# A nine-stage transformer kernel: value projections taken in pairs, and sums of squares as rounded products

## The chip, the cores and the metric

The program runs on one core of a Trainium2 chip. The metric is the device time of one execution in microseconds (us). TensorE (PE) multiplies, VectorE (DVE), ScalarE (ACT) and GpSimd (POOL) work on elements, SyncE (SP) issues most transfers. Each engine runs its own instructions in order and waits on semaphores for the others.

## The reference

512 tokens of width 1024 pass nine stages, all in float32, each after an RMS norm and added to the residual `x`: SSD and GLA (sharing one norm), SwiGLU, MLA, SwiGLU, retention, SwiGLU, stick-breaking attention, SwiGLU.

```python
def rms_norm(x, w):
    y = xf * lax.rsqrt(jnp.mean(xf * xf, axis=-1, keepdims=True) + NORM_EPS)
# MLA: 16 heads, low-rank q and kv
q = (rms_norm(cq, q_lora_norm) @ w_uq)          # per head 64 + 32 rope
kv = (rms_norm(ckv, kv_lora_norm) @ w_ukv)      # per head k 64, v 64
q_nope, q_rope, k_nope = ...                    # each normed, rope applied
p = softmax(causal(scale * (q @ k.T)));  o = p @ v
# stick-breaking: 16 heads of 64
q, k = rms_norm(q), rms_norm(k)
weight = exp(log_sigmoid(z) + later)            # later: sum of log_sigmoid(-z) over later keys
```

## The kernel before, in words

Activations lie transposed (feature on the partition, 512 tokens along the row) in eight tiles of 128x512. A float32 operand is split in a rounded high part (type fp32r) and the rest; a product is three TensorE products, high by high, high by low and low by high (`product`, L402; `features2`, L435). Other products take float32 operands as they are: among them the sums of squares of a norm (`norm`, L731, with `ones` as weights, one per 512 tokens), the mean of retention's output (L1308), MLA's k mean (L1154) and the k mean of stick-breaking (L1335).

Weights come in one stream of chunks, two in flight. SP loads chunk c into `raw` slot c % 2, POOL splits it (L716 rounds, L704 subtracts) into `w_hi`, `w_lo` once TensorE has counted the chunk before in that slot as used (`s_used`), and TensorE waits for the split.

**Norm.** ACT squares the tiles, DVE adds them into `norm_sq[:, 0]` (`squares_added`, L1872), TensorE sums over the partitions behind the next stage's first projection, ACT takes Ln and Exp (L1473, L1474).

**MLA.** Eight pairs of heads; pair u attends while pair u+1 is projected, normed and rotated. TensorE's order in a pair: `scores` of both heads (L1161 to L1166), `proj_q` (L402, 18 products), `max_turned` (L1173), `scores_turned` of head 0 (L1180 to L1185), `q_means` (L1149, L1150), `scores_turned` of head 1, `proj_k` (6 products of 512 columns), `proj_v` (24 products whose moving side is the v weight, 128 columns), `k_mean` (L1154), `weighted` twice (L1192). PSUM banks 0 to 5 hold scores and outputs, 6 and 7 the projections and means in turn. DVE norms both q heads at once: scale (L2228), two turned products for the rope (L2192), the cosine product (L2234), the sum (L2235), then k (`k_ready`, L2242), whose end lets the next `scores` start (`s_mq`). q's rstd comes from ACT, Ln per head (L1703) and one Exp for both (L1704). Before pair 0 stand the low-rank latents and their norms; DVE also fills both k buffers with the rope part (L2214) and copies four constants (L2285 to L2289).

**Retention.** Per head DVE adds four squares (L2354), and the mean is L1308.

**Stick-breaking.** Eight pairs in a like pipeline. In a pair TensorE does scores, q and k projections (banks 6, 7), `later_sums` of head 0 (L1377, L1382), `means` of the next pair (q in bank 6, L1332, L1333; k in bank 7, L1335), the first half of `proj_v` (bank 6, L1345), `later_sums` of head 1, the second half, `weighted` (bank 7, L1395), `turn_v` (L1353). DVE between the two `later_sums` splits head 1's softplus (`softplus_split`, L2406, L2407).

**End.** Once all tiles of `x` are updated (L1915) SP stores them in one transfer (L690).

Of the kernel before, what the change touches and what calls it, by code (L numbers as in the profile page):

```python
# [16 lines left out]
ALU = mybir.AluOpType  # L17
# [108 lines left out]
def weight_chunks(i, layers):  # L126
# [20 lines left out]
    for name in layers:  # L147
# [18 lines left out]
        if name == "mla":  # L166
# [4 lines left out]
            for u in range(8):  # L171
                wq = i["w_uq"][0][:, 192 * u:192 * u + 192]
                q = cols_of(*(rope_spread(wq[:, 96 * e:96 * e + 64], wq[:, 96 * e + 64:96 * e + 96]) for e in range(2)))
                q = block(q, slice(0, 384), slice(0, 256))

                kv = i["w_ukv"][0][:, 256 * u:256 * u + 256].reshape(256, 2, 2, 64).transpose(0, 2, 1, 3).reshape(256, 256)
                kv = block(kv, slice(0, 256), slice(0, 256))
                out.append(np.concatenate([q, kv], axis=1))
# [34 lines left out]
STAGE_WIDTHS = {"ssd": [384] + [2048] * 15, "gla": [2048] * 15, "mla": [2048] * 3 + [1280] * 8 + [2048] * 4,  # L213
# [65 lines left out]
def build_program(nc, x_in, weights, general_in, param_in, phase_in, out, general_at, param_at, phase_at, layers):  # L279
# [6 lines left out]
    with ExitStack() as stack:  # L286
# [168 lines left out]

        used[0] = 0
# [11 lines left out]
        def phase_const(stage, name):  # L468
# [130 lines left out]
                                                sem("mla_latent_means"), sem("mla_latent_rstd"))  # L599
        s_mkxs, s_msl = sem("mla_k_rope_square"), sem("mla_q_squares_low")  # L600
        s_mh = sem("mla_latents_normed")
# [27 lines left out]
                                                   sem("ret_mean"), sem("ret_rstd"), sem("ret_o_normed"))  # L629
        r_oo = [r_q[:, 0, :], r_q[:, 1, :], r_k[:, 0, :], r_k[:, 1, :]]  # L630
# [17 lines left out]
        k_sqh, k_sql = a_hi[:, 7, :], a_lo[:, 7, :]  # L648
# [15 lines left out]
        def _(sp):  # L664
# [61 lines left out]
        def _(pe):  # L726
            pe.sem_inc(s_used, 2)

            def norm(name):
                pe.wait_ge(s_acc, norm_of[name])  # L730
                pe.matmul(ps[:, norm_bank(name), :], ones, norm_sq[:, 0, :], start=True, stop=True).then_inc(s_mean, 1)  # L731
# [261 lines left out]
            def gla(c0):  # L993
# [104 lines left out]
                residual_begun("gla", (4, 5))  # L1098
                mean(hd)
                residual_begun("gla", range(6), 1)  # L1100

            def mla(c0):
# [26 lines left out]
                def kv_weights(par, k, at):  # L1129
                    at += 768 + 256 * k  # L1130
                    return [b[:, (c0 + 3 + par) % 2, at:at + P] for b in (w_hi, w_lo)]

                def proj_k(w, par):
                    pe.wait_ge(s_mln, 2 * w + 1)
                    product(pe, ps[:, 6, :], [(*kv_weights(par, k, 0), h_hi[:, k, :], h_lo[:, k, :])
                                              for k in range(2)]).then_inc(s_mpk, 1)

                def proj_v(w, par):
                    pe.wait_ge(s_mln, 2 * w + 2)
                    for tb in range(TB):  # L1140
                        s = slice(tb * P, (tb + 1) * P)
                        mm = product(pe, ps[:, 7, s], [(h_hi[:, k, s], h_lo[:, k, s], *kv_weights(par, k, P))
                                                       for k in range(2)])
                    mm.then_inc(s_used, 1)

                def q_means(w):
                    for e in range(2):
                        pe.wait_ge(s_msl, 2 * w + e + 1)
                        pe.matmul(ps[:, 6 + e, :], m_blkq, m_sqh[:, e, :], start=True, stop=False)  # L1149
                        pe.matmul(ps[:, 6 + e, :], m_blkq, m_sql[:, e, :], start=False, stop=True).then_inc(s_mm, 1)  # L1150
# [46 lines left out]
                def pair(u, par, first, ahead):  # L1197
# [5 lines left out]
                    pe.wait_ge(s_mv, u + 1)  # L1203
# [7 lines left out]
                    if not ahead:  # L1211
# [1276 lines left out]
```

## Time and profile before

| | |
|---|---|
| three timed runs | 2897.52, 2898.31, 2899.02 us |
| median | 2898.31 us |
| the profiled execution's own time | 2898.93 us |
| its span, first to last instruction | 2897.1 us |
| busy: TensorE, VectorE, ScalarE, GpSimd | 99%, 45%, 20%, 64% |
| mean granted TensorE clock | 0.995 |

The profile is of one execution; times in its rows count from the start of the span. A product's duration there is its way through the array and is longer than the distance from one product's start to the next one's; where products follow each other, the distance is what counts. A float32 product that is not rounded shows as two records.

### The profile page before, as it was taken

The page shows a single profiled execution, that of the slowest core. Times are in us where ns is not written, and L with a number is a line of the kernel's source. Part 1 is how long each engine was busy: PE and PEld are TensorE (multiplying, and loading weights), DVE is VectorE, ACT ScalarE, POOL GpSimd, SP SyncE. Part 2 cuts the span into 40 slices and gives each one's busy share as a digit, 9 for nine tenths or more (in the row PEclk, how much of TensorE's full clock was granted, in tenths as well). Part 3 has the DMA queues.
Part 4 walks back from the last instruction along what each step waited for, and adds up shares of the span by engine and source line. Part 5 has one row for each costly group of instructions (what it writes and reads, how often), then busy time and mean ns, then how long its engine had stood idle before and what let it go on. Part 6 is the DMA issues. An engine that isn't in the chain of part 4 may idle for free.

```text
span 2897.1 us, 36332 instructions
## 1 busy us (share of the span) xinstructions
PE 2864.6 (99%) x13536; PEld 2326.3 (80%) x13536; DVE 1301.5 (45%) x1506; ACT 565.8 (20%) x821; POOL 1848.9 (64%) x1822
## 2 busy tenths in 40 slices
PE   9999999999989999999999999999999999999998
PEld 6778888888867778888888888788888777788887
DVE  5765545414355654414444223444244455543241
ACT  4550221000124541000111101210001445300000
POOL 5557548777752238777775565677777544677775
PEclk9999999999999999999999999999999999999999
DMA  4112213232220102222232222222322111222322
GB/s 152 61 60 88 74 57 111 80 108 100 84 85 28 38 29 87 92 103 102 80 125 85 74 94 81 73 100 80 105 95 91 69 63 54 72 95 84 106 92 89
DMA packets 38583, 242.35 MB, mean 84 GB/s; under 512 B 4288, under 2 KB 4672, under 8 KB 16608
## 3 DMA queue, kind: packets, MB, share of 16 engines
q1 hardware_dynamic: 37296, 237.19, 23.5%
q10 hardware_dynamic: 1200, 3.96, 0.4%
q8 instruction: 60, 0.98, 0.1%
q14 instruction: 27, 0.22, 0.0%
HBM read 239.04 MB, written 2.10 MB: 83 GB/s over the span
## 4 chain that ended last, share of the span: by engine, by line
PE 94%; DVE 3%; ACT 1%; DVEq 1%; issue 0%; ACTq 0%; DMA 0%; SPq 0%
PE ps L402 67%; PE ps L435 13%; PE ps L1345 1%; PE ps L1161 1%; PE ps L1301 1%; PE ps L1180 1%; PE ps L1382 1%; PE ps L1362 1%; PE ps L1395 1%; PE ps L1377 1%; PE ps L1291 1%; DVEq L2262 0%; DVEq L1857 0%; PE ps L1053 0%; DVE scr L2235 0%
## 5 line engine op out<-in xcount | busy, mean ns | idle before, releaser
L716 POOL CAST w_hi<-raw 128x512 fp32r<-128x512 f32 (+1 forms) x909 | 677.5, 761 | 1030.7 <-PE ps L402 836.7
L704 POOL TENSOR_TENSOR w_lo<-raw,w_hi 128x512 fp32r<-128x512 f32 (+1 forms) x909 | 1220.0, 1354 | 0.1
L402 PE MATMUL ps<-h_hi,w_hi 128*128 128x512 f32 x1904 | 751.7, 395 | 3.3 <-DVE h_lo L1868 3.0
L402 PE MATMUL ps<-h_hi,w_lo 128*128 128x512 f32 x1904 | 742.0, 390 | 0.0
L402 PE MATMUL ps<-h_lo,w_hi 128*128 128x512 f32 x1904 | 741.5, 389 | 0.0
L402 PEld LDWEIGHTS ps<-h_hi,w_hi 128*128 128x128 f32 x1904 | 357.8, 188 | 80.8 <-issue 5.3
L402 PEld LDWEIGHTS ps<-h_hi,w_lo 128*128 128x128 f32 x1904 | 357.6, 188 | 75.7
L402 PEld LDWEIGHTS ps<-h_lo,w_hi 128*128 128x128 f32 x1904 | 357.9, 188 | 75.1 <-issue 2.9
L402 PE MATMUL ps<-a_hi,w_hi 128*128 128x512 f32 x816 | 319.7, 392 | 2.2 <-issue 1.4
L402 PE MATMUL ps<-a_hi,w_lo 128*128 128x512 f32 x816 | 318.3, 390 | 0.0
L402 PE MATMUL ps<-a_lo,w_hi 128*128 128x512 f32 x816 | 318.1, 390 | 0.0
L1896 DVE TENSOR_TENSOR scr<-ps,scr 128x512 f32<-128x512 f32 x88 | 60.9, 692 | 488.2 <-PE ps L402 423.4
L1502 ACT ACTIVATE scr<-scr 128x512 f32<-128x512 f32 x88 | 55.7, 633 | 1092.8 <-DVE scr L1896 1092.7
L1915 DVE TENSOR_TENSOR x<-ps,x 128x512 f32<-128x512 f32 x64 | 44.3, 692 | 350.3 <-PE ps L402 350.3
L1868 DVE TENSOR_TENSOR a_lo<-scr,a_hi 128x512 f32 (+1 forms) x135 | 175.0, 1296 | 18.4 <-issue 3.1
L402 PEld LDWEIGHTS ps<-a_hi,w_hi 128*128 128x128 f32 x816 | 153.6, 188 | 35.7 <-issue 3.1
L402 PEld LDWEIGHTS ps<-a_lo,w_hi 128*128 128x128 f32 x816 | 153.6, 188 | 32.1 <-issue 0.5
L402 PEld LDWEIGHTS ps<-a_hi,w_lo 128*128 128x128 f32 x816 | 153.5, 188 | 32.2
L1900 DVE TENSOR_TENSOR scr<-scr 128x512 f32<-128x512 f32 x88 | 143.3, 1629 | 14.5 <-ACT scr L1502 2.7
L402 PE MATMUL ps<-w_hi,h_hi 128*128 128x256 f32 (+1 forms) x448 | 128.9, 288 | 0.0
L402 PE MATMUL ps<-w_hi,h_lo 128*128 128x256 f32 (+1 forms) x448 | 127.4, 284 | 0.0
L402 PE MATMUL ps<-w_lo,h_hi 128*128 128x256 f32 (+1 forms) x448 | 127.3, 284 | 0.0
(319 smaller groups left out, 3614.2 us busy)
## 6 DMA issues: line engine op xcount, KB each, us to landing
raw<-weights SPq DMA_DIRECT2D x169, 1024.0 KB, 4.8
raw<-weights SPq DMA_DIRECT2D x64, 704.0 KB, 4.0
raw<-weights SPq DMA_DIRECT2D x8, 640.0 KB, 3.9
raw<-weights SPq DMA_DIRECT2D x8, 512.0 KB, 3.5
x<-x_in SPq DMA_DIRECT2D x8, 256.0 KB, 6.3
x_out<-x SPq DMA_DIRECT2D x1, 2048.0 KB, 6.3
scr<-phase_ret ACTq DMA_DIRECT2D x1, 1536.0 KB, 7.7
scr<-phase_mla ACTq DMA_DIRECT2D x1, 640.0 KB, 5.8
```

The costliest lines, as they stand in the source:

```text
L402: mm = pe.matmul(out_ap, a, b, start=(i == 0 and not begun), stop=(i == n - 1 and ended))
L435: mm = pe.matmul(ps[:, bank, :], a, b, start=(k == 0 and i == 0), stop=(k == KD - 1 and i == 2))
L704: pool.tensor_tensor(w_lo[:, slot, parts[j]], raw[:, slot, parts[j]], w_hi[:, slot, parts[j]].bitcast(F32), ALU.subtract).then_inc(s_split ...
L716: pool.tensor_copy(w_hi[:, slot, piece], raw[:, slot, piece]).then_inc(s_hi[j], 1)
L1161: pe.matmul(m_z[e][:, QO[qb]:QO[qb] + n], m_q[:, par, e, qb * P:n], m_k[:, par, e, 0:n], start=(qb != 0), stop=False, skip_group_check=True)
L1180: pe.matmul(m_z[e][:, SBO[kb]:SBO[kb] + SBW[kb]], m_k[:, par, e, kb * P:(kb + 1) * P], m_q[:, par, e, kb * P:T], start=(kb != 3), stop=Fal ...
L1291: mm = pe.matmul(ps[:, kb, 0:RW[kb]], r_k[:, k, kb * P:(kb + 1) * P], r_q[:, k, kb * P:T], start=(k == 0), stop=(k == 1))
L1502: act.activation(ffn_g[:, b, :], ffn_g[:, b, :], ACT.Silu).then_inc(s_silu, 1)
L1868: return dve.tensor_tensor(lo, src, hi.bitcast(F32), ALU.subtract)
L1896: dve.tensor_tensor(ffn_g[:, b, :], ps[:, b, :], ffn_rstd, ALU.mult).then_inc(s_gate, 1)
L1900: dve.tensor_tensor(ffn_a, ffn_g[:, b, :], ffn_u, ALU.mult)
L1915: dve.tensor_tensor(x[:, k, :], ps[:, 4 + k % 2, :], x[:, k, :], ALU.add).then_inc(s_res, 1)
```

## The change

1. Seven norms: DVE rounds `ones` into `n_ones` (128x128) and splits the summed squares into `n_hi`, `n_lo`; TensorE makes two rounded products in place of the float32 one. The same for retention's output mean (4 heads) and for the k mean of stick-breaking (8 pairs).
2. MLA's chunks carry v for two pairs: even pairs' chunks are 1536 wide (q, k, and v of two pairs), odd ones 1024 (q, k). `proj_v` makes 24 products of 256 columns for two pairs, in two parts (bank 7, then bank 6), during odd pairs only; `v_copied` on ACT takes it out in four pieces. TensorE counts an odd chunk as used after `proj_k`.
3. MLA's order: the mean of q head 0 ahead of `scores_turned` of head 0, that of head 1 and `proj_k` ahead of `scores_turned` of head 1. q's rstd goes head by head on ACT (Ln, Exp each), and DVE makes q head by head (`q_ready`), with the cosine product of one head in place of both.
4. MLA's beginning: ACT makes the constants' copies and the rope copy into the second k buffer; latents 3 and 4 are normed on either side of q head 1's squares.
5. Stick-breaking: v goes to bank 7 and the outputs to bank 6; the order is q mean, first half of v, k mean; DVE makes the low part of k's squares as well (`square_low(w, 1)`) and ACT the high part.
6. GLA: six residual products (tile 0 of the second chunk) stand ahead of the last head's mean.
7. The result is stored in eight transfers of 256 KB, each once its tile is updated.

```diff
             def norm(name):
                 pe.wait_ge(s_acc, norm_of[name])
-                pe.matmul(ps[:, norm_bank(name), :], ones, norm_sq[:, 0, :], start=True, stop=True).then_inc(s_mean, 1)
+                pe.matmul(ps[:, norm_bank(name), :], n_ones, n_hi, start=True, stop=False)
+                pe.matmul(ps[:, norm_bank(name), :], n_ones, n_lo, start=False, stop=True).then_inc(s_mean, 1)
...
-                settled().tensor_tensor(norm_sq[:, 0, :], norm_sq[:, 0, :], norm_sq[:, k, :], ALU.add)
...
+                    dve.tensor_copy(n_ones, ones)
+                    split(n_hi, n_lo, norm_sq[:, 0, :]).then_inc(s_acc, 1)
...
-            sp.wait_ge(s_res, 8 * n_res + 2)
-            sp.dma_start(out, x[:, :, :]).then_inc(s_out, 16)
+            for k in range(KD):
+                sp.wait_ge(s_res, 8 * (n_res - 1) + k + 3)
+                sp.dma_start(out[:, k, :], x[:, k, :]).then_inc(s_out, 16)
...
+                residual_begun("gla", (0,), 1)
                 mean(hd)
-                residual_begun("gla", range(6), 1)
+                residual_begun("gla", range(1, 6), 1)
...
+                def proj_v(w, part):
+                    if part == 0:
+                        pe.wait_ge(s_mln, 2 * w + 2)
+                    else:
+                        pe.wait_ge(s_mr, 3 * w + 3)
+                    for tb in (2 * part, 2 * part + 1):
                         s = slice(tb * P, (tb + 1) * P)
+                        mm = product(pe, ps[:, 7 - part, (tb % 2) * 256:(tb % 2) * 256 + 256],
+                                     [(h_hi[:, k, s], h_lo[:, k, s], *kv_weights(0, k, P, 2 * P)) for k in range(2)])
+                    mm.then_inc(s_used if part else s_mvp, 1)
...
                     scores_turned(u, par, 0)
                     if ahead:
-                        q_means(u + 1)
+                        q_mean(u + 1, 1)
+                        proj_k(u + 1, nxt)
...
                     if ahead:
-                        proj_k(u + 1, nxt)
-                        proj_v(u + 1, nxt)
+                        if par:
+                            proj_v(u + 1, 0)
                         k_mean(u + 1)
                     weighted(u, par, 0)
+                    if ahead and par:
+                        proj_v(u + 1, 1)
...
                     if ahead:
-                        means(u + 1)
+                        q_mean(u + 1)
                         proj_v(u + 1, 0)
+                        k_mean(u + 1)
```

TensorE in an MLA pair, from `max_turned` on. L1149 and L1150 are the q means before, L1159 and L1160 the same after; L1180 and L1190 are the turned scores. Before:

```order
L1173 MATMUL ps<-h_hi 128x128 x8
L1180 MATMUL ps<-scr 128x384
L1180 MATMUL ps<-scr 128x128
L1180 MATMUL ps<-scr 128x256
L1180 MATMUL ps<-scr 128x512
L1182 MATMUL ps<-h_hi 128x2x128
L1185 MATMUL ps<-h_hi 128x128 x2
L1148 ISA
L1149 MATMUL ps<-h_hi 128x512
L1150 MATMUL ps<-h_lo,h_hi 128x512
```

The same place of the change:

```order
L1159 MATMUL ps<-h_hi 128x512
L1160 MATMUL ps<-h_lo,h_hi 128x512
L1190 MATMUL ps<-scr 128x384
L1190 MATMUL ps<-scr 128x128
L1190 MATMUL ps<-scr 128x256
L1190 MATMUL ps<-scr 128x512
L1192 MATMUL ps<-h_hi 128x2x128
L1195 MATMUL ps<-h_hi 128x128 x2
L1158 REGISTER_ALU
L1159 MATMUL ps<-h_hi 128x512
L1160 MATMUL ps<-h_lo,h_hi 128x512
L403 MATMUL ps<-h_hi,w_hi 128x512
```

Head 0's mean now stands ahead of the turned scores, and `proj_k` (L403) follows head 1's mean.

ACT in the same pair, from the exponentials of head 0 (L1724 before) to those of head 1. L1703 and L1704 are Ln and Exp of q's means, L1708 and L1709 take k out and square it. Before:

```order
L1724 ACTIVATE scr<-ps 128x1280
L1702 ISA
L1703 ACTIVATE scr<-ps 128x512
L1702 REGISTER_ALU
L1703 ACTIVATE scr<-ps 128x512
L1704 ACTIVATE scr<-scr 128x1024
L1723 REGISTER_ALU
L1724 ACTIVATE scr<-ps 128x1280
L1707 REGISTER_ALU
L1708 ACTIVATE scr<-ps 128x512
L1709 ACTIVATE scr<-scr 128x512
```

The change (L1732 and L1733 are Ln and Exp of one head's mean, L1760 the exponentials, L1740 and L1741 k):

```order
L1732 ACTIVATE scr<-ps 128x512
L1733 ACTIVATE scr<-scr 128x512
L1760 ACTIVATE scr<-ps 128x1280
L1731 REGISTER_ALU
L1732 ACTIVATE scr<-ps 128x512
L1733 ACTIVATE scr<-scr 128x512
L1535 REGISTER_ALU
L1740 ACTIVATE scr<-ps 128x512
L1741 ACTIVATE scr<-scr 128x512
L1760 ACTIVATE scr<-ps 128x1280
```

Head 0's rstd is made ahead of the first exponentials, k's squares ahead of the second.

TensorE in a stick-breaking pair, after `later_sums` of head 0. Before (L1332, L1333 q mean, L1335 k mean, L1345 v):

```order
L1332 MATMUL ps<-a_hi,w_hi 128x512
L1333 MATMUL ps<-a_lo,w_hi 128x512
L1334 REGISTER_ALU
L1335 MATMUL ps<-scr,gen 128x512
L734 REGISTER_ALU
L1345 MATMUL ps<-h_hi,w_hi 128x512
L1345 MATMUL ps<-h_lo,w_hi 128x512
```

The change, the end of that stretch (L1369 v, L1358, L1359 k mean, L1401 `later_sums` of head 1):

```order
L1369 MATMUL ps<-h_hi,w_hi 128x512
L1369 MATMUL ps<-h_lo,w_hi 128x512
L1369 MATMUL ps<-h_hi,w_lo 128x512
L1356 REGISTER_ALU
L1358 MATMUL ps<-a_hi,w_hi 128x512
L1359 MATMUL ps<-a_lo,w_hi 128x512
L1401 MATMUL ps<-a_hi,a_lo 128x512
```

The k mean now stands behind v's first half, directly ahead of head 1's sums, and is two rounded products.

## Rows read from the trace of the kernel before

**Rows 1.** The page: busy time of the engines, and POOL's two costliest groups.
```profile
PE 2864.6 (99%) x13536; PEld 2326.3 (80%) x13536; DVE 1301.5 (45%) x1506; ACT 565.8 (20%) x821; POOL 1848.9 (64%) x1822
...
L716 POOL CAST w_hi<-raw 128x512 fp32r<-128x512 f32 (+1 forms) x909 | 677.5, 761 | 1030.7 <-PE ps L402 836.7
L704 POOL TENSOR_TENSOR w_lo<-raw,w_hi 128x512 fp32r<-128x512 f32 (+1 forms) x909 | 1220.0, 1354 | 0.1
```

**Rows 2.** TensorE's waits: who waited, for whom, us in total, times, longest.
```profile
PE ps L1180 <- DVE scr L2256: 2.4, 7, 0.4
PE ps L1059 <- DVE a_lo L1868: 1.6, 1, 1.6
```

**Rows 3.** Timelines at the last norm (start us, us), TensorE and then DVE.
```profile
2540.00 0.39 PE L435 MATMUL ps<-h_lo,w_hi 128*128 128x512 f32 x1
2540.23 0.39 PE L435 MATMUL ps<-h_hi,w_lo 128*128 128x512 f32 x1
...
461.33 1.02 PE L731 MATMUL ps<-scr,ones 128*128 128x512 f32 x2
...
2536.57 0.92 DVE L1872 TENSOR_TENSOR scr<-scr 128x512 f32<-128x512 f32 x1
```

**Rows 4.** Timeline of TensorE: products of 128 columns (MLA's v) and of 256.
```profile
945.67 0.27 PE L402 MATMUL ps<-w_lo,h_hi 128*128 128x128 f32 x1
...
948.13 0.28 PE L402 MATMUL ps<-w_hi,h_lo 128*128 128x128 f32 x1
...
1500.69 0.28 PE L402 MATMUL ps<-w_hi,h_hi 128*128 128x256 f32 x1
...
1501.29 0.28 PE L402 MATMUL ps<-w_hi,h_lo 128*128 128x256 f32 x1
```

**Rows 5.** Timeline of TensorE in MLA's pair 2 and at the start of pair 3.
```profile
927.64 0.59 PE L1161 MATMUL ps<-scr 128*128 128x384 f32 x1
...
938.21 1.02 PE L1180 MATMUL ps<-scr 128*128 128x384 f32 x3 [0.34 <-DVE scr L2256]
...
952.81 0.81 PE L1192 MATMUL ps<-scr 128*128 128x256 f32 x4
953.70 0.91 PE L1161 MATMUL ps<-scr 128*128 128x384 f32 x2
```

**Rows 6.** Timelines of DVE and POOL in that pair, and DVE's L2242 ahead of pair 0.
```profile
944.35 1.29 DVE L2228 SCALAR_TENSOR_TENSOR scr<-scr 128x1024 f32<-128x1024 f32 x1 [4.20 <-ACT scr L1704]
...
949.47 1.47 DVE L2235 TENSOR_TENSOR scr<-scr 48x1024 f32<-48x1024 f32 x1
951.10 2.54 DVE L2242 SCALAR_TENSOR_TENSOR scr<-scr,par 64x512 f32<-64x512 f32 x2 [0.15 <-issue]
...
948.58 2.85 POOL L716 CAST w_hi<-raw 128x512 fp32r<-128x512 f32 x2 [18.81 <-PE ps L402]
...
870.57 1.51 DVE L2242 SCALAR_TENSOR_TENSOR scr<-scr,par 64x512 f32<-64x512 f32 x2 [1.37 <-ACT scr L1474]
```

**Rows 7.** MLA ahead of pair 0: timelines, and the windows view with the granted clock.
```profile
852.79 0.70 DVE L2177 SCALAR_TENSOR_TENSOR ps<-ps,scr 128x512 f32<-128x512 f32 x1
...
857.06 0.79 PE L1149 MATMUL ps<-h_hi 128*128 128x512 f32 x1 [3.65 <-DVE h_lo L2222]
...
874.01 0.95 PE L1161 MATMUL ps<-scr 128*128 128x384 f32 x1
...
856.70:877.20 20.50, 15.44 (x43) 10.89 (x44) 12.40 (x15) 6.35 (x11) 2.81 (x5) 0.50 0.07 25
```

**Rows 8.** Timelines of DVE and TensorE in a stick-breaking pair.
```profile
2317.06 2.42 DVE L2407 TENSOR_TENSOR a_lo<-scr,a_hi 128x1280 fp32r<-128x1280 f32 x1
...
2319.87 0.39 PE L1377 MATMUL ps<-a_hi,a_lo 128*128 128x512 f32 x1
```

**Rows 9.** Transfers: count, KB each, us from issue to landing.
```profile
x_out<-x SPq DMA_DIRECT2D x1, 2048.0 KB, 6.3
...
scr<-phase_sb ACTq DMA_DIRECT2D x1, 256.0 KB, 2.7
```

More of the change, by code:

```diff
@@ L174, in weight_chunks @@
                 q = block(q, slice(0, 384), slice(0, 256))
-                kv = i["w_ukv"][0][:, 256 * u:256 * u + 256].reshape(256, 2, 2, 64).transpose(0, 2, 1, 3).reshape(256, 256)
-                kv = block(kv, slice(0, 256), slice(0, 256))
-                out.append(np.concatenate([q, kv], axis=1))
+                k, v = (i["w_ukv"][0].reshape(256, 16, 2, 64)[:, :, part].reshape(256, 1024) for part in range(2))
+                kv = [k[:, 128 * u:128 * u + 128]] + ([v[:, 128 * u:128 * u + 256]] if u % 2 == 0 else [])
+                kv = cols_of(*kv)
+                out.append(np.concatenate([q, block(kv, slice(0, 256), slice(0, kv.shape[1]))], axis=1))
             residual(i["w_o_mla"][0])
@@ L1138, in proj_v @@
-                def proj_v(w, par):
-                    pe.wait_ge(s_mln, 2 * w + 2)
-                    for tb in range(TB):
-                        s = slice(tb * P, (tb + 1) * P)
[L1142 to L1150, printed above, removed]
+                    product(pe, ps[:, 6, :], [(*kv_weights(par, k, 0, P), h_hi[:, k, :], h_lo[:, k, :])
+                                              for k in range(2)]).then_inc(s_used if par else s_mpk, 1)
@@ L1210, in pair @@
                     max_turned(u, 1)
-                    if not ahead:
+                    if ahead:
+                        q_mean(u + 1, 0)
+                    else:
                         residual_begun("mla", (2,))
@@ L1387, in weighted @@
                 def weighted(u, ahead):
-                    bank = 7 if ahead else 0
+                    bank = 6 if ahead else 0
                     pe.wait_ge(s_kv, u + 1)
@@ L1689, in mla, with q_squared @@
                 latent_squared(4, 5)
-                def q_squared(w, first=False):
+                act.activation(m_ident, phase_const("mla", "mla_ident"), ACT.Copy)
+                act.activation(m_mask, phase_const("mla", "mla_mask"), ACT.Copy)
+                act.activation(m_blkq, const("blkq"), ACT.Copy)
+                for e in range(2):
+                    act.activation(h_hi[:, 6 + e, :], x[:, e, :], ACT.Copy, scale=0.0)
+                def q_squared(w, first=False, heads=(0, 1)):
                     if not first:
                         act.wait_ge(s_mq, w)
-                    for e in range(2):
+                    for e in heads:
                         act.wait_ge(s_mpq, 2 * w + e + 1)
@@ L2435, in stick @@
                 raw(0, 1, True)
-                square_low(0)
+                for k in range(2):
+                    square_low(0, k)
                 qk_normed(0)
```

206 lines of the change are left out of this document (115 added, 91 removed).

## The prediction, made before the changed kernel was run

> **What bounds the kernel now.** I read the page first. TensorE is busy for 2864.6 of 2897.1 us [rows 1], so the kernel is TensorE's stream of products, and a change gains either by shorter products or by removing a place where TensorE stands. The second view is the list of TensorE's waits. It is short: the two entries that the change touches directly are 1.6 us before GLA's last mean and seven times 0.34 us before the turned scores of MLA [rows 2]. Since products overlap, their durations say little, so the third view is the timeline: what a product costs is the distance to the next one's start. A rounded product of 512 columns costs 0.227 us (2540.00 to 2540.23). The float32 product of a norm ends 1.02 us after 461.33, and the rounded one ahead of it, started 0.227 us earlier, ends 0.39 us after its start; so it adds 0.86 us [rows 3]. A rounded product of 128 columns costs (948.13 - 945.67) / 22 = 0.112 us, one of 256 columns (1501.29 - 1500.69) / 5 = 0.120 us [rows 4]: twice the columns for almost the same time.
>
> The fourth view is MLA's pair. Its period is 953.70 - 927.64 = 26.06 us, and two engines end it together: DVE finishes k at 951.10 + 2.54 = 953.64, and the next scores start at 953.70 [rows 5, 6]. The last products of the pair before were through TensorE's start gate some 0.28 us earlier (952.81 plus four short products of some 0.15 us each is 953.42). So a pair has 0.34 + 0.28 = 0.62 us of standing, and DVE's chain is exactly as long as TensorE's. This is the place that decides: whatever TensorE is relieved of there counts only if DVE's chain shrinks as well.
>
> **Norm sums and retention means.** Each float32 product (0.86) becomes two rounded ones (2 x 0.227 = 0.45): 0.40 us less. Seven norms give 2.8 us, four retention means 1.6 us. DVE has a cast of 128x128, a cast and a subtraction of 512 columns more ahead of the sum, about 1.5 us free and 2.6 us beside POOL (scaled from DVE's rows of that kind). The tightest norm is the last: DVE's sum ends at 2537.49 and TensorE comes 0.23 us after its product at 2540.23, so 3.0 us later [rows 3]. The cover holds with 0.4 us to spare; if it did not, the price is the difference, under 1 us for that norm. In retention 24 products of 0.227 us (5.4 us) lie between the last output product and the mean, more than DVE's addition. Nothing waits for the shorter sum but ACT, which is idle.
>
> **GLA.** Six products of 0.227 us, 1.4 us, go into a wait of 1.6 us [rows 2]. They are taken from behind the mean, where the following work is covered by 30 other products. 1.4 us less.
>
> **MLA, the work.** v costs 24 x 0.112 = 2.69 us in each pair, and 24 x 0.120 = 2.88 us in every second pair after. TensorE alone then needs, if all standing goes (head 0's mean, 0.46 us, covers the 0.34 us wait), 26.06 - 0.62 - 2.69 = 22.75 us in an even pair and 25.6 us in an odd one.
>
> **MLA, DVE's chain.** Before, DVE idles 4.20 us until 944.35 for the joint rstd, and has q ready at 951.10: 6.75 us for two heads [rows 6]. Counted from the start of the pair it was free at 940.15 - 927.64 = 12.5. Head 0's rstd is now made ahead of the first exponentials, at some 12.3, so DVE starts at 12.5. Head by head the same work needs two more drains and gets no cheaper: I take 7.3 us, an estimate, so q is ready at 19.8. k's mean comes behind the turned scores of head 1, at 10.6 + 2.5 + 0.5 + 1.4 + 2.5 = 17.4, its rstd at about 20.3. Then k takes 1.51 us (at 870.57, POOL idle) or 2.54 us (at 951.10, POOL at work) [rows 6]. Without disturbance the chain ends at 21.9, ahead of TensorE's 22.75, and in odd pairs, where k's rstd comes 1.5 us later, far ahead of 25.6.
>
> The disturbance moves, too. In an even pair the chunk of the next pair is used up by `proj_k` at about 15.3 instead of at 20.9 (948.58), so POOL begins its split in the middle of q. That chunk is the narrow one, two casts and two subtractions, 2 x (0.76 + 1.35) = 4.2 us by their means [rows 1]. From 948.58 to 953.64, with POOL at work, DVE got done what takes some 3.6 us undisturbed, 0.70 of the time. At that rate the 6.1 us that DVE has left at 15.3 end at about 23.6. The bounds are 22.75 (no disturbance, TensorE sets the end) and 12.5 + 7.3 + 1.5 + 4.2 = 25.5 (all of POOL's work adds to the chain). I take 23.6, since its rate is read from these same instructions. Seven pairs have a next one: four even ones gain 26.06 - 23.6 = 2.46 each, 9.8 us, three odd ones 0.46 each, 1.4 us. Sum 11.2 us, bounds 3.6 and 14.6.
>
> The trace shows that DVE and POOL slow each other but not to full exclusion: the two casts of POOL take 2.85 us at 948.58 and DVE's k 2.54 instead of 1.51 us [rows 6]. The Trainium skill, SBUF — State Buffer, section "SBUF: two separate sides", says that a DVE operation with two SBUF inputs and a GpSimd operation that reads SBUF take a shared port pair in turn, and that the loser blocks for the whole instruction. By that rule the even pair is nearer to 25.5; it is the second rival below.
>
> **MLA, ahead of pair 0.** TensorE stands 3.65 us until 857.06 because DVE, from 852.79 on, copies five constants before it makes the low squares, and pair 0's scores start at 874.01 [rows 7]. The copies move to ACT's idle time ahead of 852, and one rope copy of some 2 us leaves DVE as well. Walking the new order with the old durations, the low squares are done near 852.9, the latents 3 and 4 near 858.7 (862.8 before), q near 866.0, k near 867.7, and TensorE's v ends at 865.3, or at 869.6 if the clock is at half rate as before: in the 20.5 us from 856.70 the granted clock was 0.50, that is 1.2 GHz and not 2.4, after TensorE had stood [rows 7]. So pair 0 starts 4.4 to 6.2 us earlier. TensorE still stands several times there, so I expect the low clock again, and take 5.0 us. Without it up to 1.5 us more.
>
> **Stick-breaking.** On TensorE's side the k mean saves 0.40 us a pair and no longer waits for ACT (0.2 us). But it stands between the two `later_sums`, and the second waits for DVE's split, which ends at 2317.06 + 2.42 = 2319.48 while TensorE starts at 2319.87 [rows 8]. DVE gets one more subtraction (0.69 us, up to 1.1 beside POOL) just ahead of that split, of which its idle time hides most; the rest, 0.1 to 0.5 us, moves the split's end to 2319.6 to 2320.0. TensorE gains 0.2 us or loses 0.2 us a pair. Seven pairs: -1.2 to +1.4 us, I take 0. The means' saving is lost to a new wait, on DVE.
>
> **The store.** The one transfer lands 6.3 us after its issue, one of 256 KB with other contents 2.7 us [rows 9]. Seven of the eight go out during the last products, so the end comes 3.5 us earlier (2.5 to 4 for a store with shorter rows).
>
> **Sum.** 2.8 + 1.6 + 1.4 + 11.2 + 5.0 + 0 + 3.5 = 25.5 us off the profiled execution's 2898.93, which is 2873.4. That execution was 0.6 us above the median of the timed runs, so I forecast 2872.8 us.
>
> **Rivals.** First, TensorE stays the bound in all of MLA and stick-breaking gains its 1.2: 2.8 + 1.6 + 1.4 + 14.6 + 6.2 + 1.2 + 3.5 = 31.3, or 2867.0 us. For it speaks that POOL's split is short and DVE has 0.9 us in hand. Second, DVE and POOL exclude each other, by which even pairs last 25.5 and stick-breaking loses 2: 2.8 + 1.6 + 1.4 + 3.6 + 4.4 - 2.1 + 3.5 = 15.2, or 2883.1 us. Against it speaks the 0.70 above. Third, the change does not do what it says in the loop: q's rstd is not ready early (head 0's mean comes late, or ACT is behind), DVE still sets 26.06 us a pair, and the shorter v is only longer standing: 25.5 - 11.2 = 14.3, or 2884 us. Fourth, on the other side: the low clock. Standing of TensorE at the end of even pairs brings it back to 1.2 GHz, as standing did ahead of pair 0. A stretch of 20.5 us at half rate costs at most 10.2 us where TensorE is the bound, so from three such stretches on (2872.8 + 30.7 = 2903.5 us) the kernel is slower. Against it: pairs with 0.62 us of standing kept the full clock, and I expect about 0.9.
>
> **Chances.** The forecast 0.50, first rival 0.26, second 0.12, third 0.06, fourth 0.02, and 0.04 for mixtures that end within the noise of the old time. The range of 8 in 10 takes the forecast, the first rival with the clock kept high (2864) and most of the second: 2864 to 2882.5. A measurement of this kernel can tell about 0.2%, 5.8 us, so faster means below 2892.5: 0.95; same 0.03; slower 0.02.
>
> **What would show it.** In the changed profile: TensorE's products of 256 columns in MLA at 0.12 us distance, 96 of them, and none of 128; even pairs of 23 to 24 us with a wait of up to 1 us for DVE at the scores' start, odd ones of 25.6 with none; pair 0's scores 4 to 6 us earlier relative to the end of the MLA norm; stick-breaking's period still near 29.3 us, with a wait of TensorE for DVE at the second `later_sums`; the last transfer landing some 3 us after its issue. I am wrong if even pairs wait for something else than DVE's k, above all for ACT, or if the seven norms begin to show waits.

## The result, and the profile after

The changed kernel takes 2884.18 us in the median of five runs (2879.98 to 2884.34), the kernel before 2898.54 us; the ratio is 0.9946, interval 0.9931 to 0.996. It is faster by 14.4 us, where the prediction said 25.5 and its range ended at 2882.5 us. The profiled execution took 2884.22 us, 14.7 less than the profiled one of before.

The page of the changed kernel, busy time, and its transfers of the result (count, KB each, median us to landing):

```profile
PE 2849.0 (99%) x13440; PEld 2315.1 (80%) x13440; DVE 1347.6 (47%) x1578; ACT 573.4 (20%) x851; POOL 1838.7 (64%) x1814
...
x_out<-x SPq DMA_DIRECT2D x8, 256.0 KB, 5.2
```

TensorE's busy time fell by 15.6 us against [rows 1], DVE's rose by 46. The list of TensorE's waits (who, for whom, us in total, times, longest) has these entries, among others:

```profile
PE ps L1171 <- DVE scr L2287: 7.3, 4, 3.5
PE ps L1401 <- DVE a_lo L2448: 3.8, 7, 0.5
...
PE ps L1352 <- DVE a_lo L2426: 1.8, 1, 1.8
...
PE ps L1358 <- ACT scr L1840: 0.7, 1, 0.7
PE ps L403 <- POOL w_lo L710: 0.5, 1, 0.5
PE ps L737 <- DVE a_lo L1916: 0.4, 1, 0.4
```

L1171 is `scores` in MLA, L1401 `later_sums`, L1352 and L1358 the q and k means of stick-breaking. The list of before has none of them but the q mean's, which was shorter:

```profile
PE ps L1332 <- DVE a_lo L2386: 1.4, 1, 1.4
```

New waits for DVE have come in where work of DVE was added or moved.

Where the time went is read from the starts of the seven norm sums (L731 before, L737 after) on TensorE's timeline. Before, and then after, in part:

```profile
821.27 0.59 PE L731 MATMUL ps<-scr,ones 128*128 128x512 f32 x1
...
1127.72 0.59 PE L731 MATMUL ps<-scr,ones 128*128 128x512 f32 x1
...
2258.38 0.59 PE L731 MATMUL ps<-scr,ones 128*128 128x512 f32 x1
```

```profile
462.56 0.50 PE L737 MATMUL ps<-a_hi 128*128 128x512 f32 x1
...
822.93 0.39 PE L737 MATMUL ps<-a_hi 128*128 128x512 f32 x1
...
1116.51 0.39 PE L737 MATMUL ps<-a_hi 128*128 128x512 f32 x1
...
2244.04 0.39 PE L737 MATMUL ps<-a_hi 128*128 128x512 f32 x1
...
2530.33 0.50 PE L737 MATMUL ps<-a_hi 128*128 128x512 f32 x1 [0.38 <-DVE a_lo L1916]
```

| stretch | before | after | difference | forecast |
|---|---|---|---|---|
| start to GLA's first mean (code unchanged) | 291.17 | 293.73 | +2.6 | 0 |
| from there to the first norm sum | 170.16 | 168.83 | -1.3 | -1.4 |
| first norm sum to MLA's | 359.94 | 360.37 | +0.4 | -0.4 |
| MLA's norm sum to the next | 306.45 | 293.58 | -12.9 | -16.6 |
| three norm stretches with retention | 1130.66 | 1127.53 | -3.1 | -2.8 |
| stick-breaking's norm sum to the last | 282.08 | 286.29 | +4.2 | -0.4 |
| last norm sum to the end | 356.65 | 352.08 | -4.6 | -3.9 |
| whole span | 2897.1 | 2882.4 | -14.7 | -25.5 |

Four rows carry the error: 2.6 us at the start, 0.8 at the first norm, 3.7 in MLA and 4.6 in stick-breaking. The end gives 0.7 back.

**The start is not the change's.** The windows view of all engines, 185 to 205 us (length, busy time of TensorE, its loads, DVE, ACT and POOL, granted clock, DMA share, GB/s): before, after, and the kernel with one store, told of below.

```profile
185.00:205.00 20.00, 19.69 (x73) 13.94 (x72) 8.34 (x12) 5.88 (x7) 8.11 (x8) 0.91 0.18 68
```

```profile
185.00:205.00 20.00, 19.69 (x66) 13.11 (x65) 7.53 (x10) 3.34 (x5) 8.09 (x8) 0.83 0.23 88
```

```profile
185.00:205.00 20.00, 19.69 (x81) 14.10 (x80) 9.62 (x14) 7.25 (x8) 8.15 (x8) 1.00 0.20 73
```

In the same instructions the clock sank to 1.2 GHz for 3.4, for 6.8 and for 0 us. Over the eleven profiles of the changed kernel and its variants the first norm sum stands at 458.7 to 458.8 us (four) or at 462.0 to 462.9 us (seven). So one execution can be 4 us longer than the next without any difference of code. The medians carry this as well, and not evenly: of 37 timed executions of the kernel before four took 2901.6 or 2901.7 us, 2.7 above its profiled one, while of the changed kernel's five four are at 2883.8 to 2884.3 us, the profiled one with its 6.8 us of low clock among them, and one is at 2880.0. So the 14.4 us between the medians most likely hold these 2.6 us too. Whether the changed program meets the longer start more often, or chance did it, is not shown. The stretches of the trace below leave the start out. With the same code in MLA its stretch still varied by 0.4 us (293.20 to 293.58 in five profiles). Where both are given, the stretch decides.

**MLA.** TensorE's timeline, the start of pairs 0, 1, 2 and 3, then of 6 and 7:

```profile
870.07 0.48 PE L1171 MATMUL ps<-scr 128*128 128x384 f32 x1
...
893.96 0.59 PE L1171 MATMUL ps<-scr 128*128 128x384 f32 x1 [1.17 <-DVE scr L2287]
...
919.54 0.49 PE L1171 MATMUL ps<-scr 128*128 128x384 f32 x1
...
943.77 0.59 PE L1171 MATMUL ps<-scr 128*128 128x384 f32 x1 [1.47 <-DVE scr L2287]
...
1018.77 0.49 PE L1171 MATMUL ps<-scr 128*128 128x384 f32 x1
...
1045.00 0.59 PE L1171 MATMUL ps<-scr 128*128 128x384 f32 x1 [3.46 <-DVE scr L2287]
```

Even pairs take 23.89, 24.23, 23.98 us, and pair 6 takes 26.23; odd ones 25.5 to 25.6. The three ordinary even pairs are within 0.7 us of the forecast 23.6, the odd ones at their 25.6. Pair 6 is not. DVE and POOL there:

```profile
1036.29 2.62 DVE L2241 TENSOR_TENSOR scr<-scr 16x512 f32<-16x512 f32 x2
1038.93 1.66 DVE L2279 TENSOR_TENSOR scr<-scr 128x512 f32<-128x512 f32 x1
...
1041.75 3.19 DVE L2287 SCALAR_TENSOR_TENSOR scr<-scr,par 64x512 f32<-64x512 f32 x2 [0.15 <-issue]
```

```profile
1034.03 1.64 POOL L722 CAST w_hi<-raw 128x512 fp32r<-128x512 f32 x2 [9.25 <-PE ps L403]
...
1041.02 3.38 POOL L710 TENSOR_TENSOR w_lo<-raw,w_hi 128x512 fp32r<-128x512 f32 x2
```

POOL works there from 1034.0 to 1044.4 us, four casts and four subtractions, because the next chunk in that slot is no longer one of MLA's narrow ones but the first of the full width for the residual. DVE's k takes 3.19 us, where it took 1.51 us in pair 2, after POOL had finished at 939.34:

```profile
942.20 1.51 DVE L2287 SCALAR_TENSOR_TENSOR scr<-scr,par 64x512 f32<-64x512 f32 x2 [0.15 <-issue]
...
935.95 3.39 POOL L710 TENSOR_TENSOR w_lo<-raw,w_hi 128x512 fp32r<-128x512 f32 x2
```

In pair 6 TensorE stands 3.46 us, and behind it the clock sank to 1.2 GHz for 3.4 us from 1046.3 on.

**Stick-breaking.** DVE ahead of the second `later_sums`, and TensorE there:

```profile
2302.78 1.19 DVE L2426 TENSOR_TENSOR a_lo<-scr,a_hi 128x512 fp32r<-128x512 f32 x1 [1.22 <-ACT scr L1836]
2304.05 1.06 DVE L2447 CAST a_hi<-scr 128x1280 fp32r<-128x1280 f32 x1
2305.19 2.42 DVE L2448 TENSOR_TENSOR a_lo<-scr,a_hi 128x1280 fp32r<-128x1280 f32 x1
```

```profile
2286.59 0.69 PE L1386 MATMUL ps<-scr 64*128 64x512 f32 x1
...
2307.67 0.50 PE L1401 MATMUL ps<-a_hi,a_lo 128*128 128x512 f32 x1 [0.55 <-DVE a_lo L2448]
...
2316.20 0.70 PE L1386 MATMUL ps<-scr 64*128 64x512 f32 x2
```

The period is 2316.20 - 2286.59 = 29.61 us against 29.3 before, so the loop lost 1.9 us. Ahead of the loop, from the norm sum to pair 0's scores, it is 13.00 us (2244.04 to 2257.04) against 11.28: the waits of 1.8 us (1.4 before) and 0.7 us, and behind them a low clock of 3.4 us in which twelve products took 4.34 us and not 2.72. The last norm's wait of 0.38 us is most of the rest.

### The profile page after: what moved, and what is told of

It reads as the page before. It is cut to its first block, busy times and chain, and to the rows that moved or that the text cites. A ratio compares the mean times of both kernels' runs of the same rounds, so it can differ in the third digit from the quotient of the medians.

```text
span 2882.4 us, 36314 instructions
## 1 busy us (share of the span) xinstructions
PE 2849.0 (99%) x13440; PEld 2315.1 (80%) x13440; DVE 1347.6 (47%) x1578; ACT 573.4 (20%) x851; POOL 1838.7 (64%) x1814
## 4 chain that ended last, share of the span: by engine, by line
PE 92%; DVE 4%; POOL 1%; ACT 1%; DVEq 1%; issue 1%; DMA 0%; ACTq 0%; SPq 0%; POOLq 0%
PE ps L403 68%; PE ps L436 12%; PE ps L1171 1%; PE ps L1320 1%; PE ps L1369 1%; PE ps L1386 1%; POOL w_lo L710 1%; PE ps L1419 1%; PE ps L1190 1%; PE ps L1202 1%; PE ps L1310 1%; DVE a_lo L2448 1%; POOL w_hi L722 0%; PE ps L1406 0%; PE ps L1401 0%
## 5 line engine op out<-in xcount | busy, mean ns | idle before, releaser
L722 POOL CAST w_hi<-raw 128x512 fp32r<-128x512 f32 (+1 forms) x905 | 666.8, 753 | 1030.5 <-PE ps L403 829.1
L403 PE MATMUL ps<-h_hi,w_hi 128*128 128x512 f32 x1904 | 747.4, 393 | 2.2 <-DVE h_lo L1916 1.4
L403 PE MATMUL ps<-h_hi,w_lo 128*128 128x512 f32 x1904 | 741.8, 390 | 0.0
L403 PE MATMUL ps<-h_lo,w_hi 128*128 128x512 f32 x1904 | 741.5, 389 | 0.0
L403 PEld LDWEIGHTS ps<-h_hi,w_hi 128*128 128x128 f32 x1904 | 357.8, 188 | 77.9 <-issue 3.6
L403 PEld LDWEIGHTS ps<-h_hi,w_lo 128*128 128x128 f32 x1904 | 357.7, 188 | 75.0
L403 PEld LDWEIGHTS ps<-h_lo,w_hi 128*128 128x128 f32 x1904 | 357.9, 188 | 73.7 <-issue 0.7
L403 PE MATMUL ps<-a_hi,w_hi 128*128 128x512 f32 x816 | 320.0, 392 | 2.2 <-issue 1.4
L403 PE MATMUL ps<-a_hi,w_lo 128*128 128x512 f32 x816 | 318.3, 390 | 0.0
L403 PE MATMUL ps<-a_lo,w_hi 128*128 128x512 f32 x816 | 318.2, 390 | 0.0
L1916 DVE TENSOR_TENSOR a_lo<-scr,a_hi 128x512 f32 (+1 forms) x146 | 186.2, 1275 | 17.5
L403 PEld LDWEIGHTS ps<-a_hi,w_hi 128*128 128x128 f32 x816 | 153.7, 188 | 36.7 <-issue 3.8
L403 PEld LDWEIGHTS ps<-a_lo,w_hi 128*128 128x128 f32 x816 | 153.8, 188 | 32.0 <-issue 0.5
L403 PEld LDWEIGHTS ps<-a_hi,w_lo 128*128 128x128 f32 x816 | 153.6, 188 | 32.1
L436 PE MATMUL ps<-a_hi,w_hi 128*128 128x512 f32 x320 | 125.6, 392 | 0.0
L436 PE MATMUL ps<-a_hi,w_lo 128*128 128x512 f32 x320 | 124.6, 389 | 0.0
L436 PE MATMUL ps<-a_lo,w_hi 128*128 128x512 f32 x320 | 124.6, 389 | 0.0
```

Of the source, the lines that this page charges most:

```text
L403: mm = pe.matmul(out_ap, a, b, start=(i == 0 and not begun), stop=(i == n - 1 and ended))
L436: mm = pe.matmul(ps[:, bank, :], a, b, start=(k == 0 and i == 0), stop=(k == KD - 1 and i == 2))
L722: pool.tensor_copy(w_hi[:, slot, piece], raw[:, slot, piece]).then_inc(s_hi[j], 1)
L1916: return dve.tensor_tensor(lo, src, hi.bitcast(F32), ALU.subtract)
```

## The experiments

My theory after the comparison: both losses have one form, POOL's split of the next chunk running beside DVE at the moment that TensorE is about to wait for DVE. The rivals were that DVE's chain is too long even alone, and that the new order or banks cost the time.

**1. Stick-breaking undone.** Only this stage goes back to its old form in all three engines:

```diff
-                        q_mean(u + 1)
-                        proj_v(u + 1, 0)
-                        k_mean(u + 1)
+                        means(u + 1)
+                        proj_v(u + 1, 0)
```

> The changed kernel (2884.2 us) with stick-breaking alone as before (v's place and bank, the float32 k mean, DVE's and ACT's parts). Theory A: the stage as changed costs 4.6 us. From its norm to the next stage's norm it takes 286.28 us changed, against 282.07 before less 0.40 for the norm: 2879.6 us here, period back at 29.30, no wait of TensorE for DVE at the second later_sums. Theory B: the stage's change is worth nothing by itself, as forecast, and what differs comes from elsewhere: 2884 us.

Measured 2880.34 us (ratio 0.9949), 3.8 below the changed kernel. Norm to norm 282.57 us, period 29.30, lead-in 11.24 us. So the stage's change costs 3.7 us. That is 0.9 less than theory A said: this kernel too waits 0.37 us at the last norm, and its lead-in is only 0.04 us shorter than before the change and not 0.4, since TensorE waits there for DVE.

**2. Only the rounding of the k mean undone.**

```diff
-                    pe.wait_ge(s_ksl, 2 * w + 2)
-                    pe.matmul(ps[:, 6, :], k_blk, k_sqh[:, 1, :], start=True, stop=False)
-                    pe.matmul(ps[:, 6, :], k_blk, k_sql[:, 1, :], start=False, stop=True).then_inc(s_kmean, 1)
+                    pe.wait_ge(s_ksq, 2 * w + 2)
+                    pe.matmul(ps[:, 6, :], const("blk64"), k_sq[:, 1, :], start=True, stop=True).then_inc(s_kmean, 1)
```

> The changed kernel with only the rounding of stick-breaking's k mean undone: it stays behind the first half of v and in bank 6, but is one float32 product, and DVE does not make the low part of k's squares. TensorE has 0.40 us more in a pair, DVE 1.19 us less ahead of the split. Theory A (the extra subtraction is what makes the split late): the wait of 0.55 us and the slow start behind it (0.3) go, period 29.2 instead of 29.61, and the lead-in loses its 1.8 us wait: 2879 to 2880.5 us. Theory B (the new place of the mean and v's new bank cost the time): period stays near 29.6, 2884 us.

Measured 2881.45 us, norm to norm 284.04 (2.25 less), period 29.19: the longer product is the cheaper one, because DVE's subtraction is gone. Theory A holds for the loop. For the lead-in it fell: it took 13.45 us, with the same waits of 1.8 and 0.7 us and the same low clock.

**3. A later release in stick-breaking.** No work changes; TensorE counts the q and k chunk as used 5.8 us later (DVE's wait for k goes by a count of its own).

```diff
-                    features(pe, ps[:, 7, :], c0 % 2, 256, P, P).then_inc(s_used, 1)
+                    features(pe, ps[:, 7, :], c0 % 2, 256, P, P).then_inc(s_mpk, 1)
...
-                    pe.matmul(ps[:, 6, :], k_blk, k_sqh[:, 1, :], start=True, stop=False)
+                    mm = pe.matmul(ps[:, 6, :], k_blk, k_sqh[:, 1, :], start=True, stop=False)
+                    if release:
+                        mm.then_inc(s_used, 1)
```

> The changed kernel with one thing moved in stick-breaking: TensorE counts the q and k chunk as used at the k mean instead of at the end of proj_k, 5.8 us later, so that POOL's split of the next chunk begins behind most of DVE's softplus split. No work is added or taken. Theory A (POOL's work beside DVE makes the split late: 1.19, 1.06 and 2.42 us instead of 0.69, 0.83 and 1.49): the split ends 1.6 us earlier, the wait of TensorE goes, period 28.8 instead of 29.61, 2878.3 us. Theory B (DVE has too much work there even when alone): period 29.6, 2884 us. Theory C: the disturbance moves to q's and k's norming behind it, and the next scores wait: between the two, or over 2884.

Measured 2874.29 us (ratio 0.9928), norm to norm 280.37: 5.9 less. DVE and POOL in that kernel:

```profile
2297.91 0.69 DVE L2430 TENSOR_TENSOR a_lo<-scr,a_hi 128x512 fp32r<-128x512 f32 x1 [1.22 <-ACT scr L1838]
2298.69 0.83 DVE L2451 CAST a_hi<-scr 128x1280 fp32r<-128x1280 f32 x1
2299.59 1.49 DVE L2452 TENSOR_TENSOR a_lo<-scr,a_hi 128x1280 fp32r<-128x1280 f32 x1
```

```profile
2302.20 1.17 POOL L722 CAST w_hi<-raw 128x512 fp32r<-128x512 f32 x2 [16.37 <-PE ps L1358]
```

The same three instructions take 3.01 us where they took 4.67, and POOL's split now starts behind them. TensorE's wait is gone and the period is 28.73 us (forecast by theory A: 28.8), 0.57 below the kernel before.

**4. A later release in MLA.** In even pairs the odd pair's chunk is released at the last `weighted`:

```diff
-                                              for k in range(2)]).then_inc(s_used if par else s_mpk, 1)
+                                              for k in range(2)]).then_inc(s_mpk, 1)
...
+                        if used and kb == 0:
+                            mm.then_inc(s_used, 1)
...
-                    weighted(u, par, 1)
+                    weighted(u, par, 1, ahead and not par)
```

> The changed kernel with one thing moved in MLA: in even pairs the odd pair's chunk is counted as used at the last weighted product's start instead of at proj_k, some 6 us later, so that POOL's split (four casts and subtractions in pair 6, two in the others) runs behind DVE's q and k. No work is added or taken. Theory A (POOL's work beside DVE is the whole wait of even pairs): pairs 0, 2, 4 take 22.8 instead of 23.9 to 24.2, pair 6 22.8 instead of 26.1, the low clock after pair 6 goes (1.6): 2875.6 us. Theory B (DVE's chain is too long by itself, or waits for ACT): even pairs stay near 24 and pair 6 near 26, 2884 us.

Measured 2873.5 us (ratio 0.9914); norm to norm 283.49, 10.1 less (theory A: 8.6). All four even pairs take 22.56 to 22.58 us, L1171 has left the list of waits, and the low clock behind pair 6 is gone. TensorE's timeline (the starts of pairs 0, 1 and 3), and DVE's k in pair 2, which now ends 0.60 us ahead of the scores at 941.13:

```profile
870.57 0.48 PE L1171 MATMUL ps<-scr 128*128 128x384 f32 x1
...
893.15 0.49 PE L1171 MATMUL ps<-scr 128*128 128x384 f32 x1
...
941.13 0.81 PE L1171 MATMUL ps<-scr 128*128 128x384 f32 x2
```

```profile
939.02 1.51 DVE L2286 SCALAR_TENSOR_TENSOR scr<-scr,par 64x512 f32<-64x512 f32 x2 [0.15 <-issue]
```

A later release also moves the transfer that refills `raw`. It isn't what slows DVE: in the changed kernel's trace the 46 float32 operations of DVE with two inputs of 128x512 in SBUF that ran without POOL took 0.69 us each, 12 of them while transfers ran, and those beside POOL 0.9 to 1.8 us, half of them 1.6 or more.

**5. Both releases.** The diffs of experiments 3 and 4 together (DVE's count in stick-breaking starts at 8 instead of 4, as MLA's eight pairs have raised it).

> Both late releases together (MLA's odd chunk and stick-breaking's q and k chunk), nothing else. Theory A (the two losses are separate places, each its stage's own): the savings add, 10.1 us in MLA (293.58 to 283.5 from norm to norm) and 5.9 in stick-breaking (286.29 to 280.4): 2868.2 us. Theory B (they share a cause, such as the clock or the weight stream): less than the sum, 2870 to 2874 us. The stretch from the start to the first of the seven norms, whose code none of these kernels changes, took 462.1 to 462.9 us in profiles with a low clock of 6.8 us at 193 us and 458.7 to 458.8 in profiles without: it is expected at one of the two again, and moves the total by 4 us whatever the kernel.

Measured 2868.19 us (ratio 0.9893, 0.9878 to 0.9908); 283.52 and 280.36 us in the two stretches. They add; theory A.

**6. The ones by ACT**, in the kernel of experiment 5:

```diff
+                    if k == KD - 1:
+                        act.activation(n_ones, ones, ACT.Copy)
                     act.activation(norm_sq[:, k, :], x[:, k, :], ACT.Square).then_inc(s_sq, 1)
...
-                    dve.tensor_copy(n_ones, ones)
```

> As the kernel with both late releases, and n_ones is made by ACT ahead of the squares of the last tile instead of by DVE between the last addition and the split. Theory A (at the first of the seven norms the extra DVE work, of which that copy took 1.31 us beside POOL, is what TensorE and POOL wait for): from that norm to MLA's norm 359.5 us instead of 360.4, as at the other stages of this kind; the wait of 0.4 us at the norm's first product goes: 2867.3 us. Theory B (the 0.9 us belong to POOL's split alone): 360.4 stays, 2868.2 us.

Measured 2867.7 us. The first stretch stays at 360.48: theory B. Its rows of TensorE:

```profile
462.33 0.39 PE L737 MATMUL ps<-a_hi 128*128 128x512 f32 x1
462.56 0.39 PE L738 MATMUL ps<-a_lo,a_hi 128*128 128x512 f32 x1
463.64 0.49 PE L403 MATMUL ps<-h_hi,w_hi 128*128 128x512 f32 x1 [0.70 <-POOL w_lo L710]
```

The sum now comes on time and TensorE only stands longer behind it, for POOL. That names the cause: in the timeline of before, POOL's two subtractions there take 2.53 us (459.31 to 461.84) and end 0.15 us ahead of TensorE's need (461.99); beside DVE's new split they take 2.96 to 3.15 us, and the shorter sum brings the need forward. At the last norm the copy did matter: the wait of 0.38 us has left the list, and the stretch is 0.27 us shorter (280.36 to 280.09). Some of it stays, as the sum starts 0.44 us behind the product ahead of it and not 0.23. My expectation had placed that wait at the first norm, while it was the last one's.

**7. Stick-breaking's lead-in, v first.**

```diff
                 proj_v(0, 0, 3)
+                proj_v(0, 1, 3)
                 q_mean(0)
-                k_mean(0, False)
-                proj_v(0, 1, 3)
+                k_mean(0, False, 7)
+                pe.wait_ge(s_kr, 1)
```

(and on DVE `v_scaled(0, 3)` ahead of `qk_normed(0)`)

> As the one before, and stick-breaking's beginning reordered: all of v's products ahead of both means of pair 0, k's mean in bank 7 so that it does not wait for ACT's Ln of q's, v's scaling on DVE ahead of the norming. Theory A (the two waits of 1.8 and 0.7 us and the low clock of 3.4 us behind them, 1.6 us on 12 products, are the lead-in's loss): first scores 10 to 10.4 us behind the norm instead of 13.0, 2864.7 us. Theory B (DVE's and ACT's chain sets the end and TensorE stands later instead, with the low clock on the scores): 12 to 13 us, 2866.5 to 2867.3 us.

Measured 2867.03 us, norm to norm 279.29 (0.8 less). Scores start at 10.75 us instead of 13.0, but TensorE stands ahead of them and the low clock falls on pair 0, which takes 30.21 us and not 28.73. Theory B.

**8. One store**, in the changed kernel:

```diff
-            for k in range(KD):
-                sp.wait_ge(s_res, 8 * (n_res - 1) + k + 3)
-                sp.dma_start(out[:, k, :], x[:, k, :]).then_inc(s_out, 16)
-            sp.wait_ge(s_out, 16 * KD)
+            sp.wait_ge(s_res, 8 * n_res + 2)
+            sp.dma_start(out, x[:, :, :]).then_inc(s_out, 16)
+            sp.wait_ge(s_out, 16)
```

> The changed kernel with only the store undone: one transfer of 2 MB at the end. Theory A (the eight stores' gain is the landing time alone, 6.3 us for 2 MB against 2.0 us for the last 256 KB): from the last norm to the end 356.2 us instead of 352.07, 2888.3 us. Theory B (the bound of the prediction, 3.5 us): 2887.7 us.

From the last norm sum to the end 356.35 us against 352.08: 4.3 us, theory A. The median, 2884.46 us (2884.22 to 2888.6), shows only 0.3 of it; this kernel's profiled execution has no low clock at the start (third row of the windows above), which hides 4 us, and its two longer runs are at 2885.8 and 2888.6. By the median alone the experiment is inconclusive.

**9 and 10. What brings the low clock in the lead-in.** Both start from experiment 6. First the k mean of pair 0 alone goes to bank 7, without the wait for ACT; then that mean is also one float32 product, so that this lead-in is the old one:

```diff
-                k_mean(0, False)
+                k_mean(0, False, 7)
```

```diff
-                k_mean(0, False, 7)
+                pe.wait_ge(s_ksq, 2)
+                pe.matmul(ps[:, 7, :], const("blk64"), k_sq[:, 1, :], start=True, stop=True).then_inc(s_kmean, 1)
```

> As the kernel with both releases and ones by ACT, with v's order in stick-breaking's beginning as changed (half of v, the two means, the other half), and only the k mean of pair 0 in bank 7, as it stood before the change, so that it does not wait for ACT's Ln of q's. Theory A (the second wait, 0.7 us directly behind the first of 1.8, is what brings the low clock): no low clock there, first scores 11.2 us behind the norm as before the change instead of 13.0, first pair 28.7: 2865.9 us against the 2867.7 of the kernel it starts from. Theory B (the wait of 1.8 us alone brings it): low clock of 3.4 us stays on v's second half, 12.3 us, 2867 us.

> As the kernel with the k mean of pair 0 in bank 7, and that one mean is again one float32 product, without DVE's low part of its squares, as before the change; the seven means of the loop stay rounded. Theory A (it takes the 1.8 us wait and then a further gap of 0.3 to 0.7 us behind q's mean to bring the low clock; with the float32 product right behind q's mean there is none): no low clock there, first scores 11.2 us behind the norm instead of 12.6, 278.3 us from norm to norm instead of 279.67, some 2865 us. Theory B (the wait of 1.8 us alone brings it, and that one kernel ran without it was chance): low clock on v's second half, 12.8 us, 2866.5 us.

Measured 2866.4 us (ratio 0.9886) and 2863.17 us (0.9877, 0.9861 to 0.9893), with lead-ins of 12.60 and 12.47 us and the low clock in both: theory B in both. Between the two profiled executions lie 4.7 us, of which 4.0 are the start (458.65 us to the first norm sum against 462.62), and 0.16 the stretch. The windows of TensorE on v's second half, experiment 10 and then experiment 1 (which has the same order of products there):

```profile
2236.00:2240.00 4.00, 4.00 (x11) 0.57 0.21 41
```

```profile
2245.60:2249.60 4.00, 3.66 (x15) 1.00 0.10 16
```

TensorE did the same thing ahead of both windows, twelve products, a wait of 1.8 us, the q mean and the float32 mean, and once the clock fell and once it did not. Of ten profiles with a wait of 1.8 us at the q mean nine show the low clock behind it and experiment 1 doesn't; the kernel before waited 1.4 us there and doesn't either. So these profiles can't tell whether the change lost the 1.6 us of the low clock there or chance did. This stays open.

## Why the prediction was wrong

**Holds.** What bounds the kernel; the price of a rounded sum (the stretches without other changes went from 359.94 to 359.5, 0.44 us, forecast 0.40); retention and GLA; the odd pairs (25.5 to 25.6 for 25.6); TensorE's own bound in even pairs (22.56 in experiment 4, forecast 22.75, slightly pessimistic); DVE's chain there without disturbance (21.96 us in experiment 4, 918.57 to 940.53, forecast 21.9); MLA's lead-in: pair 0 starts 47.14 us behind the norm sum instead of 52.74, 5.6 us, of which 0.4 is the norm, so 5.2 for 5.0. That last match is in part luck: the low clock came back, as forecast, but for 10.2 us and not for 20.5.

**Fails, MLA's loop, 2.3 us and 1.6 behind it.** The step is "That chunk is the narrow one, two casts and two subtractions". For pair 6 it is not: the next chunk in that slot belongs to the residual and is full width. The program's table of chunk widths has it, 1536 and 1024 in turn for the eight pairs and then 2048 again; I had walked pair 2 and multiplied it by four. Pair 6 took 2.6 us more than forecast, and the low clock behind it cost 1.6.

The other three even pairs took 1.3 us more together, and here the sum was wrong: "At that rate the 6.1 us that DVE has left at 15.3 end at about 23.6" should read 15.3 + 6.1 / 0.70 = 24.0. They took 24.03 us in the mean, but that the 24.0 fits is luck: POOL worked for only 4.54 us in pair 2 (934.80 to 939.34), and in these DVE lost 2.2 us (its k ends 24.17 us behind the pair's start, against 21.96 in experiment 4), so its rate there was about 0.5 and not 0.70. Against these losses 1.5 us came unforeseen: the forecast counted 26.06 us for every pair before, and pair 0, which began in the low clock [rows 7], took 27.58 (874.01 to 901.59):

```profile
901.59 0.59 PE L1161 MATMUL ps<-scr 128*128 128x384 f32 x1
```

**Fails, stick-breaking, 4.6 us.** What the prediction said of DVE is about right. The rows before, the start of the pair of [rows 8] on TensorE and the cast ahead of the split on DVE:

```profile
2298.94 0.70 PE L1362 MATMUL ps<-scr 64*128 64x512 f32 x2
...
2315.79 1.20 DVE L2406 CAST a_hi<-scr 128x1280 fp32r<-128x1280 f32 x1 [1.89 <-PE ps L1382]
```

Counted from the pair's start the split ended at 20.54 us and ends at 21.02, 0.48 later, within the forecast 0.1 to 0.5; the idle time hid most of the extra subtraction's 1.19 us. The step that fails is "TensorE gains 0.2 us or loses 0.2 us a pair", of which I took 0. The split's end came at the late end of its range, so the sums start at 21.08 us and not at 20.93. And a wait costs more than its own length, which no term had: behind the 0.55 us the first product takes 0.34 us to the next start (2307.67 to 2308.01) and not 0.227, and some 0.13 us more are lost. Together that is 0.28 us a pair.

The lead-in was not walked at all in this stage and so stood at nothing, though the change gave it a second wait (0.7 us) and DVE's second subtraction; it took 1.7 us more, most of it the low clock, whose cause stays open (experiments 9 and 10). My first rival's 1.2 us gain here was possible only with a later release, which gives 0.57 us a pair.

**Fails, the norms.** The step is "The cover holds with 0.4 us to spare". DVE's extra work was put at 2.6 us beside POOL and measured 3.4 us (1.31, 1.38 and 0.69 at the last norm), against a cover of 3.0: 0.38 us of waiting there. At the first norm I asked only what waits for DVE, not what DVE slows: POOL's split was 0.15 us ahead of need.

**Fails, the store,** by its size: 3.5 us forecast, 4.2 by the stretch without its norm and 4.3 in experiment 8. I had gone by 2.7 us, a load of the same size; the stores of the changed kernel, by their line, and the last of them is the 2.0:

```profile
L696 SPq DMA_DIRECT2D x_out<-x x8: 332/387/1137, 2855.3 to 2880.0; - x8
...
DMA to landing us min/median/max: 2.0/5.2/5.6
```

**Not foreseen:** 2.6 us at the start, in unchanged code, where executions differ without any difference of code. Without it the kernel would have shown about 2881.6 us, within the range and still 8.8 us short.

Two rivals' numbers are near the result, 2883.1 and 2884, and neither by its mechanism. The second has even pairs of 25.5 us, and the ordinary ones took 23.9 to 24.2. The third has q's rstd late, and in pair 2 DVE starts on q 12.50 us behind the pair's start, as forecast, without waiting for ACT.

On the Trainium skill, SBUF — State Buffer, section "SBUF: two separate sides", the runs now say more. Beside POOL a DVE subtraction with two SBUF inputs took 2.42 us and not 1.49, and k's two instructions took 3.19 us and not 1.51, and both came back when POOL's work alone was moved (experiments 3 and 4). But full exclusion is not what pair 2 shows: in the 4.54 us of POOL's work there POOL did what takes some 3.8 us beside an idle DVE, and DVE what takes about 1.9 us beside an idle POOL, together more than the time.

## What to carry to other kernels

When a buffer's release starts work on an engine that disturbs another, the moment of release is a knob of its own: counting two chunks as used some 6 us later, with no work changed, gained 16 us, more than the whole change. No run tries the later releases in the kernel before, so how much of this is loss that the change itself had brought is not shown. Walk the last turn of every loop, as its buffers are refilled for other work. A shorter product that needs one more step on another engine is a gain only if that step has cover; the longer float32 mean was faster here. The version with both late releases, the ones by ACT and the old first k mean has the lowest median, 2863.17 us, 0.9877 of the kernel before; but some 4 us of its lead on experiment 5 are the shorter start, and by the stretches it gained about 0.9 us in stick-breaking (280.36 to 279.51).

## What the runs showed of the hardware

The clock sank to 1.2 GHz in the same unchanged stretch (192 to 200 us) for 0, 3.4 or 6.8 us in different executions, and behind the same sequence of TensorE in one execution and not in another. In MLA 3.46 us of standing ahead of pair 7 brought it, the waits of 1.2 to 1.5 us at pairs 1, 3 and 5 did not; at stick-breaking's q mean 1.8 us of standing came ahead of it in nine profiles and not in a tenth.

POOL slows DVE's work between SBUF tiles: a cast of 128x128 took 1.31 us beside POOL, where its like takes 0.22 us alone, and a float32 operation with two inputs of 128x512 took 0.9 to 1.8 us instead of 0.69. Operations of the same size with one input in PSUM kept 0.67 to 0.70 us beside POOL, in all 396 cases of the changed kernel's trace that ran beside it for more than half of their time.
